# Modulation blocks in groups of four instead of two, in the gate-up chunks and the last down projection of a two-block transformer kernel

## The chip, the cores and the metric

The kernel runs on one core of one Trainium2 chip. The metric is the device time of one execution in microseconds (us). Engines: PE is TensorE (matmuls), ACT ScalarE, DVE VectorE, POOL GpSimd, SP the engine whose queue issues the weight DMAs.

## What is computed

Two model blocks run one after the other on 256 tokens of width 1024. The first has two layers (mixer, then a gated feed-forward network). The second has two layers whose norm is shifted, scaled and gated by "modulation" vectors. These depend only on two conditioning vectors, not on the tokens, so the kernel computes them while the first block is running. Cut to what matters:

```python
def hybrid_layer(x, ...):                       # first block, twice
    h = rms_norm(x, g_mix_pre)
    z = h @ w_in                                # mixer: retention, attention, gated MLP
    ...
    x = x + rms_norm(y @ w_out, g_mix_post)
    h = rms_norm(x, g_ffn_pre)
    gate, up = split(h @ w_gate_up, [FFN_HIDDEN])   # 1024 x 5632
    f = (silu(gate) * up) @ w_down                  # 2816 x 1024
    return x + rms_norm(f, g_ffn_post)

# second block, layer l: the modulation
mod_l = silu(c) @ w_mod[l] + b_mod[l]           # w_mod[l]: 1024 x 3072
mod_c = silu(c_ctx) @ w_mod[l] + b_mod[l]
sh, sc, g = split(mod, 3)                       # shift, scale, gate: the "thirds" 0, 1, 2
h = rmsnorm(x, norm_g[l]) * (1 + sc) + sh
```

## The kernel before

**Weights** come in one fixed order through a ring of 8 raw slots in SBUF, 512 KB each (`RAW = 8`). A piece of weights in a slot is a "granule". `ring` (filled at L357 to L411) is the order of the DMAs, which all stand in SP's queue: `load` (L434) issues the DMA of ring place i when the granule of place i − 8 has left its slot.

**Two kinds of granules.** A projection granule is cut into a high and a low part, so that three fast matmuls (high by high, low by high, high by low) stand for one of full precision. ACT writes the high part (`cut_high`, L447), DVE the low part (`cut_low`, L459), in ring order, three granules ahead of PE at most; four pairs of cut slots (`CUT = 4`) come free as PE finishes granules. The raw slot is free once the low part is cut. A modulation block (`add_mod`, L380) is one of eight 128-row input blocks of `w_mod` for one third. It is not cut: PE multiplies with the raw slot itself (`mod_rows_pe`, L985: four matmuls of 32 columns a block, recorded as 8), and the slot is free only when PE has done that (`mods_done`).

**Gate-up** (L3058 on): eleven chunks c of four granules h each. For each granule PE makes 12 matmuls of 512 columns (two token tiles, three products, two row blocks). At c ≥ 1, behind the granule h = 1, PE turns the f of chunk c − 1 (`turn_f`, L3047 to L3057, four transposes), after waiting for DVE to have formed it (`gate`, L2891 to L2903), which in its turn waits for ACT's tanh (`gate_tanh`, L2735 to L2743). In ACT's and DVE's order, tanh and gate of chunk c − 1 stand at the start of chunk c, which is behind the cut of the granule (c, 2): cuts run three granules ahead.

**Where modulation stands.** `MOD_AT` (L363) names granules (c, h) in gate-up at which blocks of third 0 stand. In the ring they come ahead of that granule (L377), on PE behind its matmuls (L3063). `MOD_LAST` (L388) names the down-projection granules n of layer 1 ahead of which blocks of third 2 stand, in the ring (L406) and on PE (L3091). Third 1 is at other places, in groups of four, among them the group of four behind the first gate-up chunk's second granule, and is not touched. When all eight blocks of third 0 are done, ACT copies the rows out (`mod_rows_act`, at c = 5), and DVE sums the gate rows at n = 10 of the last down projection.

**Other DMAs** near it: in layer 1, POOL fetches `ctx_raw` (1024 KB) when chunk 0 is done and `const_late` (1154 KB) when granule (2, 3) is done (L2660 to L2664).

Of the kernel before, what the change touches and what calls it, by code (L numbers as in the profile page):

```python
# [173 lines left out]
def program(nc, a, out, tables):  # L174
    where = Where()
    ctx = ExitStack()
    with ctx:
# [182 lines left out]
        PAIRS = [(2 * h, 2 * h + 1) for h in range(DK // 2)]  # L360
        IN_COLS = ((Z_GU, 2 * GMW), (Z_AQ, RW), (Z_AK, RW), (Z_AV, RW), (Z_RQ, RW), (Z_RK, RW), (Z_RV, RW), (Z_RG, RW))
        IN_CHUNKS, GU_CHUNKS = len(IN_COLS), FK // 2
        MOD_AT = {(2, 1): (0, 1), (2, 3): (2, 3), (4, 1): (4, 5), (4, 3): (6, 7)}  # L363
        w_in, w_out, w_gu, w_down, w_mods = [], [], [], [], {}

        def pre_gain(at, layer, rows):
            return vec_cols[:, at + layer * DK + rows[0]:at + layer * DK + rows[-1] + 1]
# [6 lines left out]
        def add_gu(layer, chunks):  # L374
            for c in chunks:
                for h, rows in enumerate(PAIRS):
                    if (c, h) in MOD_AT:  # L377
                        add_mod(layer, 0, MOD_AT[c, h])
                    w_gu[layer].add_split(a["w_gate_up"][layer], rows, c * SEQ, SEQ, pre_gain(V_FFN, layer, rows))

        def add_mod(layer, third, ks):
            ph = w_mods.setdefault((layer, third), Phase(f"mod{third}"))
            for k in ks:
                ph.add(a["w_mod_2"][layer], (k,), D * third, D, cut=False)


        FIRST_KS, LAST_KS = range(0, 4), range(4, 8)
        MOD_LAST = {4: (0, 1), 5: (2, 3), 7: (4, 5), 8: (6, 7)}  # L388
        MIX_ORDER = [(j, PAIRS[h]) for hs in ((2, 3), (1, 0)) for j in range(2) for h in hs]
        OUT_ORDER = [(j, PAIRS[h]) for hs in ((0, 1), (2, 3)) for j in range(2) for h in hs]  # L390
        for layer in range(DEPTH):
# [3 lines left out]
        for layer in range(DEPTH):  # L395
# [9 lines left out]
            for n in range(FK):  # L405
                if last and n in MOD_LAST:  # L406
                    add_mod(layer, 2, MOD_LAST[n])
                w_down[layer].add(a["w_down"][layer], (n,), 0, D)
# [573 lines left out]
        def gate_rows_bank(layer):  # L982
            return 5 if layer == DEPTH - 1 else 6

        def mod_rows_pe(e, third, ks, bank, parts=1):  # L985

            if third == 1 and ks[0] == 0:
                e.wait_ge(dve.sem, dve.value("ret_centred"))
            part = DK // parts
            for k in ks:  # L990
                g = w_mods[where.layer, third].granules[k]
                e.wait_ge(landed[g.slot], g.landed)
                for q in range(4):
                    last = e.matmul(PS[32 * q:32 * q + 32, bank, 0:SEQ], silu_c[:, k, :], g.raw[:, 0, q * SEQ:(q + 1) * SEQ],  # L994
                                    start=k % part == 0, stop=k % part == part - 1)
                last.then_inc(mods_done, 1)
# [1988 lines left out]
        def pe_layer(e, layer, cuts):  # L2985
# [63 lines left out]
            def turn_f(c):  # L3049

                e.wait_ge(dve.sem, dve.value(f"f{c}"))
                if c >= 2:
                    e.wait_ge(dve.sem, dve.value(f"f_L{c - 2}"))
                for kk in range(2):
                    for t in range(NT):
                        last = e.transpose(PS[:, TP[c % 2], kk * SEQ + t * P:kk * SEQ + (t + 1) * P],  # L3056
                                           f[:, c % 2, t, kk * P:(kk + 1) * P], ident)  # L3057
                last.then_inc(pe.sem, pe.mark(f"f_T{c}"))  # L3058
            for c in range(1, GU_CHUNKS):
                for h in chunk_pe(e, w_gu[layer].granules[4 * c:4 * c + 4], "gate_up", c, hT, MM[c % 2], lambda t: free_f(c)):  # L3060
                    if h == 1:
                        turn_f(c - 1)
                    if (c, h) in MOD_AT:  # L3063
                        mod_rows_pe(e, 0, MOD_AT[c, h], MOD_BANKS[0, 0])
                    elif (c, h) == (6, 2):
# [22 lines left out]
            for n, g in enumerate(g_down[:-4]):  # L3088
                if n == 2:
                    turn_f(GU_CHUNKS - 1)  # L3090
                if layer == DEPTH - 1 and n in MOD_LAST:  # L3091
                    mod_rows_pe(e, 2, MOD_LAST[n], gate_rows_bank(layer))
                if layer == DEPTH - 1 and n == 13:
# [55 lines left out]
def build(nc, arrays, tables):  # L3149
    a = {k: nc.dram_tensor(k, v.shape, mybir.dt.from_np(v.dtype), kind="ExternalInput").ap()  # L3150
         for k, v in arrays.items()}
    out = nc.dram_tensor("out", (1, SEQ, D), F32, kind="ExternalOutput").ap()
    program(nc, a, out, tables)
# [14 lines left out]
```

## Time and profile before

| | before |
|---|---|
| median of 3 runs | 1066.53 us (1066.33 to 1068.08) |
| profiled execution | 1066.61 us, span of the core 1064.7 us |
| granted TensorE clock, mean | 0.997 |
| PE busy | 1037.4 us, 97% |
| DVE, ACT, POOL busy | 64%, 52%, 8% |
| weight DMAs (queue q1) | 161.96 MB, 47.4% of the 16 DMA engines |
| `w_mod` DMAs | 48 of 512 KB each |
| L994 (modulation matmuls) | 384 records |

The page also gives the chain of work that ended last: PE has 87% of it. A row of a timeline reads: start, duration, engine, line, operation, written <- read tiles, how many were merged, and in brackets the idle time before it with what ended it. Matmuls overlap: the distance between the starts is what one costs. In a row of windows the last three numbers are the granted clock (1.00 is full), the busy share of the DMA engines and GB/s.

### The profile page before, as it was taken

How to read it: one execution, taken by the hardware profiler on the slowest of the kernel's cores; microseconds unless marked ns; L12 is line 12 of the kernel's file. 1: busy time of each engine (PE TensorE's matmuls, PEld its weight loads, DVE VectorE, ACT ScalarE, POOL GpSimd, SP SyncE). 2: the span in 40 equal slices, each digit the busy share in tenths (PEclk: the TensorE clock that was granted, in tenths of full speed). 3: DMA queues.
4: the chain of work that ended last, by engine and by line, in shares of the span. 5: the costliest groups of instructions: out<-in, count | busy, mean ns of one | idle time of the engine just before them, and what ended most of it. 6: DMA issues, size and time to landing. Idle time of an engine off the chain costs nothing.

```text
span 1064.7 us, 15796 instructions
## 1 busy us (share of the span) xinstructions
PE 1037.4 (97%) x6070; PEld 875.3 (82%) x6070; DVE 683.5 (64%) x1202; ACT 549.4 (52%) x998; POOL 83.9 (8%) x102
## 2 busy tenths in 40 slices
PE   7999999999999999999999999999998999999997
PEld 6899777788887999777788788899985678889785
DVE  5995676666546896675666357433457734986665
ACT  6665365555435565364655355334345734543772
POOL 2000110000002100110000001001000002220130
PEclk9999999999999999999999999999999999999999
DMA  9645576766666755586866585133131021542001
GB/s 346 204 144 163 192 258 222 247 205 188 190 195 233 225 155 163 193 284 214 296 222 187 188 302 154 45 102 122 60 99 38 1 80 40 178 158 80 2 2 40
DMA packets 103828, 170.75 MB, mean 160 GB/s; under 512 B 7365, under 2 KB 70866, under 8 KB 103498
## 3 DMA queue, kind: packets, MB, share of 16 engines
q1 hardware_dynamic: 101524, 161.96, 47.4%
q0 software_dynamic: 1696, 6.38, 1.9%
q10 hardware_dynamic: 534, 1.41, 0.3%
q8 instruction: 48, 0.79, 0.3%
q14 instruction: 26, 0.21, 0.1%
HBM read 168.21 MB, written 1.05 MB: 159 GB/s over the span
## 4 chain that ended last, share of the span: by engine, by line
PE 87%; DVE 7%; ACT 2%; issue 2%; DMA 1%; SPq 0%; DVEq 0%; POOLq 0%; POOL 0%; ACTq 0%
PE PS L492 17%; PE PS L497 16%; PE PS L493 16%; PE PS L3077 4%; PE PS L3081 4%; PE PS L3078 4%; PE PS L994 2%; PE PS L1873 2%; PE PS L960 1%; DVE low L462 1%; PE PS L961 1%; PE PS L965 1%; PE PS L1861 1%; PE PS L1984 1%; PE PS L3056 1%
## 5 line engine op out<-in xcount | busy, mean ns | idle before, releaser
L462 DVE TENSOR_TENSOR low<-raw,high 128x1024 fp32r<-128x1024 f32 (+3 forms) x182 | 202.3, 1117 | 167.1 <-ACT high L452 166.0
L492 PE MATMUL PS<-high,hT_high 128*128 128x512 f32 (+2 forms) x796 | 302.7, 381 | 0.3 <-ACT high L452 0.3
L493 PE MATMUL PS<-high,hT_low 128*128 128x512 f32 (+2 forms) x796 | 296.2, 372 | 0.0
L452 ACT ACTIVATE high<-raw 128x1024 fp32r<-128x1024 f32 (+3 forms) x186 | 179.3, 972 | 209.3 <-PE PS L497 114.9
L497 PE MATMUL PS<-low,hT_high 128*128 128x512 f32 (+2 forms) x796 | 231.9, 372 | 0.9 <-DVE low L465 0.9
L492 PEld LDWEIGHTS PS<-high,hT_high 128*128 128x128 f32 x796 | 150.2, 189 | 27.5 <-issue 5.1
L497 PEld LDWEIGHTS PS<-low,hT_high 128*128 128x128 f32 x796 | 147.5, 189 | 23.5 <-DVE low L465 2.1
L493 PEld LDWEIGHTS PS<-high,hT_low 128*128 128x128 f32 x796 | 150.5, 189 | 19.5
L465 DVE SCALAR_TENSOR_TENSOR low<-raw,vec_cols,high 128x512 fp32r<-128x512 f32 x176 | 123.7, 747 | 61.4 <-ACT high L455 61.4
L455 ACT ACTIVATE high<-raw,vec_cols 128x512 fp32r<-128x512 f32 x176 | 117.1, 715 | 59.4 <-PE PS L497 34.6
L3077 PE MATMUL PS<-high,fT_high 128*128 128x512 f32 x176 | 69.5, 395 | 0.0
L3078 PE MATMUL PS<-high,fT_low 128*128 128x512 f32 x176 | 68.7, 390 | 0.0
L3081 PE MATMUL PS<-low,fT_high 128*128 128x512 f32 x176 | 68.6, 390 | 0.0
L492 PE MATMUL PS<-high,cT_high 128*128 128x512 f32 (+2 forms) x124 | 45.2, 366 | 0.0
L493 PE MATMUL PS<-high,cT_low 128*128 128x512 f32 (+2 forms) x124 | 45.0, 365 | 0.0
L3077 PEld LDWEIGHTS PS<-high,fT_high 128*128 128x128 f32 x176 | 33.1, 188 | 8.3 <-issue 1.6
L3081 PEld LDWEIGHTS PS<-low,fT_high 128*128 128x128 f32 x176 | 33.1, 188 | 7.0
L3078 PEld LDWEIGHTS PS<-high,fT_low 128*128 128x128 f32 x176 | 33.1, 188 | 6.6
L497 PE MATMUL PS<-low,cT_high 128*128 128x512 f32 (+2 forms) x124 | 35.5, 365 | 0.0
L2433 DVE CUSTOM_DVE_ANT_0 z_late<-PS,consts 128x512 f32<-128x512 f32 x32 | 22.8, 749 | 15.8 <-PE PS L1995 15.8
L1962 ACT ACTIVATE z_late<-z_late,consts 128x512 f32<-128x512 f32 x32 | 22.9, 716 | 18.9 <-DVE consts L2433 18.9
L2747 ACT ACTIVATE fT_high<-PS 128x512 fp32r<-128x512 f32 x22 | 13.1, 598 | 37.5 <-PE PS L3056 37.5
(380 smaller groups left out, 1578.4 us busy)
## 6 DMA issues: line engine op xcount, KB each, us to landing
raw<-w_gate_up SPq DMA_DIRECT2D x176, 256.0 KB
raw<-w_mod SPq DMA_DIRECT2D x48, 512.0 KB
raw<-w_down SPq DMA_DIRECT2D x44, 512.0 KB
raw<-w_in SPq DMA_DIRECT2D x56, 384.0 KB
raw<-o_w_in SPq DMA_DIRECT2D x20, 512.0 KB
raw<-w_out SPq DMA_DIRECT2D x16, 512.0 KB
raw<-e_w_in SPq DMA_DIRECT2D x12, 512.0 KB
raw<-w_in SPq DMA_DIRECT2D x8, 512.0 KB
```

Of the source, the lines that this page charges most:

```text
L452: last = e.activation(g.high, g.raw, ACT.Copy)
L455: last = e.activation(g.high[:, i, :], g.raw[:, i, :], ACT.Copy, scale=g.gain[:, i:i + 1])
L462: last = e.tensor_tensor(g.low, g.raw, g.high.bitcast(F32), ALU.subtract)
L465: last = e.scalar_tensor_tensor(g.low[:, i, :], g.raw[:, i, :], g.gain[:, i:i + 1], g.high[:, i, :].bitcast(F32), ALU.mult, ALU.subtract)
L492: e.matmul(bank, xh[:, k, tokens], g.high[:, i, :], start=first and i == 0, stop=False)
L493: e.matmul(bank, xl[:, k, tokens], g.high[:, i, :], start=False, stop=False)
L497: done = e.matmul(bank, xh[:, k, tokens], g.low[:, i, :], start=False, stop=last and i == len(g.rows) - 1)
L1962: e.activation(o_prob[:, i % 4, :], o_logits[i % 4], ACT.Exp, bias=e_neg[:, i:i + 1], scale=-1.0, accum_out=e_den[:, i:i + 1]).then_inc(ac ...
L2433: e.tensor_tensor_reduce(o_logits[i % 4], PS[:, i % 2, :], late_const("window", NT)[:, t, :], -1.0, neg_sink[:, h:h + 1], ALU.add, ALU.min ...
L3077: e.matmul(bank, fT_high[:, n, tokens], g.high[:, 0, cols], start=n == 0, stop=False)
L3078: e.matmul(bank, fT_low[:, n, tokens], g.high[:, 0, cols], start=False, stop=False)
L3081: last = e.matmul(bank, fT_high[:, n, tokens], g.low[:, 0, cols], start=False, stop=n == FK - 1)
```

## The change

Two tables change. In `MOD_AT` the four groups of two blocks in the gate-up of each layer, at granules (2, 1), (2, 3), (4, 1) and (4, 3), become two groups of four at (2, 2) and (4, 2). In `MOD_LAST` the four groups of two in layer 1's down projection, at granules 4, 5, 7 and 8, become two groups of four at 5 and 8. The order of DMAs in SP's queue and the order of matmuls on PE follow from the same tables. Every block is still loaded and multiplied once, in the same order among themselves, into the same PSUM banks.

```diff
-        MOD_AT = {(2, 1): (0, 1), (2, 3): (2, 3), (4, 1): (4, 5), (4, 3): (6, 7)}
+        MOD_AT = {(2, 2): (0, 1, 2, 3), (4, 2): (4, 5, 6, 7)}
...
-        MOD_LAST = {4: (0, 1), 5: (2, 3), 7: (4, 5), 8: (6, 7)}
+        MOD_LAST = {5: (0, 1, 2, 3), 8: (4, 5, 6, 7)}
```

## Rows read from the trace of the kernel before

**Rows 1.** The page, part 1: engine, busy us, share of the span, instructions.
```profile
PE 1037.4 (97%) x6070; PEld 875.3 (82%) x6070; DVE 683.5 (64%) x1202; ACT 549.4 (52%) x998; POOL 83.9 (8%) x102
```
**Rows 2.** Waits of PE: who waited for whom, us in total, times, longest; then that wait's end.
```profile
PE PS L1065 <- DVE gel L1319: 2.9, 2, 2.2
...
51.11 1.22 PE L1065 MATMUL PS<-gel,wsT 128*128 128x128 f32 x4 [2.18 <-DVE gel L1319]
```
**Rows 3.** Timeline of PE, layer 0, chunks 2 and 3: turns, visits of two, granule starts.
```profile
166.98 0.60 PE L3056 MATMUL PS<-consts,f 128*128 128x128 f32 x4
...
171.38 0.39 PE L492 MATMUL PS<-high,hT_high 128*128 128x512 f32 x1
...
174.19 1.07 PE L994 MATMUL PS<-raw,silu_c 128*32 128x256 f32 x16
175.19 0.50 PE L492 MATMUL PS<-high,hT_high 128*128 128x512 f32 x1
...
178.09 0.39 PE L492 MATMUL PS<-high,hT_high 128*128 128x512 f32 x1
...
180.81 0.60 PE L3056 MATMUL PS<-consts,f 128*128 128x128 f32 x4
...
184.02 0.39 PE L492 MATMUL PS<-high,hT_high 128*128 128x512 f32 x1
```
**Rows 4.** Timeline of PE, layer 0, chunk 0: a visit of four blocks (third 1).
```profile
141.77 1.93 PE L994 MATMUL PS<-raw,silu_c 128*32 128x256 f32 x32
143.63 0.50 PE L492 MATMUL PS<-high,hT_high 128*128 128x512 f32 x1
```
**Rows 5.** Timeline of PE, layer 1, down projection: two visits with a granule between.
```profile
600.35 1.07 PE L994 MATMUL PS<-raw,silu_c 128*32 128x256 f32 x16
...
604.33 1.07 PE L994 MATMUL PS<-raw,silu_c 128*32 128x256 f32 x16
```
**Rows 6.** Timeline of SP, layer 1: the DMA issues behind the first visit.
```profile
487.82 3.95 SPq L444 DMA_DIRECT2D raw<-w_gate_up  x8
```
**Rows 7.** Timeline of PE, layer 1: first turn and visit, and chunk 3's turn.
```profile
486.60 0.60 PE L3056 MATMUL PS<-consts,f 128*128 128x128 f32 x4
487.12 1.07 PE L994 MATMUL PS<-raw,silu_c 128*32 128x256 f32 x16
...
511.80 0.60 PE L3056 MATMUL PS<-consts,f 128*128 128x128 f32 x4
```
**Rows 8.** Timeline of ACT, layer 1: cuts that waited for a DMA.
```profile
491.44 1.34 ACT L455 ACTIVATE high<-raw,vec_cols 128x512 fp32r<-128x512 f32 x2 [3.62 <-DMA raw<-w_gate_up]
...
505.73 2.66 ACT L455 ACTIVATE high<-raw,vec_cols 128x512 fp32r<-128x512 f32 x4 [4.07 <-DMA raw<-w_gate_up]
...
510.92 1.34 ACT L455 ACTIVATE high<-raw,vec_cols 128x512 fp32r<-128x512 f32 x2 [1.81 <-DMA raw<-w_gate_up]
...
612.40 1.06 ACT L452 ACTIVATE high<-raw 128x1024 fp32r<-128x1024 f32 x1 [3.01 <-DMA raw<-w_down]
```
**Rows 9.** Timeline of DVE, layer 1: the last step of chunk 3's f.
```profile
510.48 0.87 DVE L2902 SCALAR_TENSOR_TENSOR f<-f,norms,PS 128x256 f32<-128x256 f32 x2
```
**Rows 10.** Windows, us: busy by engine, clock, DMA share, GB/s; layer 1, then layer 0.
```profile
487.00:511.00 24.00, 24.00 (x131) 18.65 (x130) 12.29 (x20) 10.62 (x19) 1.09 (x2) 1.00 0.93 309
188.00:192.00 4.00, 4.00 (x20) 3.30 (x19) 3.30 (x7) 1.98 (x4) 0.00 (x0) 1.00 0.00 1
```
**Rows 11.** DMA queues from 494 to 504 us: packets, MB, share of 16 engines.
```profile
q0 software_dynamic: 176, 1.19, 46.5%
```
**Rows 12.** Windows behind PE's wait near 51 us.
```profile
51.10:54.50 3.40, 3.39 (x13) 3.40 (x14) 3.33 (x7) 1.26 (x2) 0.00 (x0) 0.50 0.40 116
54.50:58.00 3.50, 3.50 (x26) 3.47 (x26) 3.44 (x8) 1.97 (x4) 0.00 (x0) 1.00 0.45 119
```
**Rows 13.** Timelines of layer 0: the burst's second landing (ACT), chunk 3's turn (PE).
```profile
174.50 1.34 ACT L455 ACTIVATE high<-raw,vec_cols 128x512 fp32r<-128x512 f32 x2 [1.44 <-DMA raw<-w_gate_up]
...
192.18 0.60 PE L3056 MATMUL PS<-consts,f 128*128 128x128 f32 x4
```

## Prediction

> **What bounds the kernel now.** I read the page's busy times first: TensorE (PE) 97% busy, the vector and scalar engines far from that [rows 1]. Its waits, second, are few: the longest inside the run is 2.18 us at one place near 51 us [rows 2]. In the stretches that the change touches, the PE timeline has one matmul behind the other: from 178.09 to 180.81 us a "granule" (one 512 KB weight block: two token tiles by six matmuls) takes 2.72 us [rows 3]. So PE sets the end there. But the SP queue, the cuts on ACT and the DMA windows show that its cover is thin in one spot. That spot decides this change.
>
> All times are those of the profiled execution: span 1064.7 us, 1066.61 us with what lies around it; the median of the runs shown is 1066.53, so I take 0.1 off at the end. "g(c,h)" is granule h of gate-up chunk c, "m0" to "m7" are the eight modulation blocks of a phase.
>
> **The change, part by part.** Nothing is computed more or less: 48 blocks of modulation rows stand in the kernel before and after. In each layer's gate-up, two visits of PE with two blocks each (behind g(2,1) and g(2,3), and behind g(4,1) and g(4,3)) become one visit with four, behind g(2,2) and g(4,2). In the last down projection four visits become two.
>
> *A visit's price.* The first of a pair comes behind the turn of f (L3056), a visit of its own: from L3056 to the second granule's start 171.38 − 166.98 = 4.40 us; less 2.72 for the granule, 1.68. The turn alone costs 184.02 − 180.81 − 2.72 = 0.49 [rows 3], so these two blocks add 1.19. The second costs 178.09 − 171.38 − 2 × 2.72 = 1.27 [rows 3]. A visit of four is in the trace too, behind the first gate-up chunk: 143.63 − 141.77 = 1.86 us from its first matmul to the next granule's [rows 4], where two blocks take 175.19 − 174.19 = 1.00 [rows 3]. Two more blocks thus cost 0.86, and a visit of four 1.27 + 0.86 = 2.13. A merge in gate-up gives 1.19 + 1.27 − 2.13 = 0.33; there are four (two per layer): 1.3 us. In the down projection a visit costs 604.33 − 600.35 − 2.72 = 1.26 [rows 5], a merge gives 2 × 1.26 − 2.12 = 0.40, two of them 0.8. PE gains **2.1 us** in all.
>
> *What is moved in the queues.* A block's DMA into raw slot i may only be issued when the granule eight places earlier in the ring has left its slot. A weight granule leaves when DVE has cut it, some three granules ahead of PE; a modulation block leaves only when PE has multiplied with it. So SP stands at m0 until PE gets there, and everything behind m0 in SP's queue stands too. In layer 1 before: the turn starts at 486.60, m0's matmuls at 487.12, and SP sends a burst from 487.82 on, 0.70 us after them [rows 6, 7]. Afterwards g(2,2) stands between turn and m0: 486.60 + 0.49 + 2.72 + 0.09 (the entry: 174.19 − 171.38 − 2.72 [rows 3]) = 489.90 for m0, and the burst starts at 490.60, **2.78 us later**. And since four blocks now lie together, the order behind it changes. Before: g(3,1), g(3,2), g(3,3), g(4,0), m4, m5, g(4,1), g(4,2): g(4,2) is the 8th of the burst. After: g(3,2), g(3,3), g(4,0), g(4,1), m4 to m7, g(4,2): it is the **9th**.
>
> *Who waits for g(4,2).* ACT cuts its high part and only then takes chunk 3's tanh (L2742); DVE cuts its low part and only then forms f of chunk 3 (L2897, L2902); and PE turns that f (L3056) behind g(4,1), ahead of everything else. So its landing is behind the next turn, though no matmul of the granule itself is due. In layer 1 before, ACT waited for DMA until 505.73, when the 7th, g(4,1), came, and again until 510.92 for the 11th, g(4,3) [rows 8]: 5.19 / 4 = 1.30 us a block. The 8th hence landed near 507.03. f of chunk 3 was ready at 510.48 + 0.87 = 511.35 [rows 9], 4.32 us after that landing, and PE reached the turn at 511.80 [rows 7]: **0.45 us of margin**. Afterwards PE comes 0.33 earlier, 511.47. The 9th of a burst landed at 505.73 + 2 × 1.30 = 508.33, and 2.78 later is 511.11. f is ready at 515.43. PE waits **3.9 to 4.0 us**.
>
> *Bounds of that wait.* Low: the DMA engines were 0.93 busy over the whole burst [rows 10], partly with const_late, which POOL fetches at the end of chunk 2. If every block took 1.30 us behind a first landing 491.44 − 487.82 = 3.62 us after issue [rows 6, 8], and const_late (1154 KB) 2.25 such shares, the 9th would land at 490.60 + 3.62 + 10.4 + 2.9 = 507.5 and the wait would be 0.4 us. High: one more share of 1.30, if const_late, which does not move with the burst, gets in the way more: 5.3 us. I take 3.9, because the same queue with the same guest has shown just this rate at this place.
> The Trainium skill says (DMA: Bandwidth & Descriptors, "Issuing engines are not separate DMA queues") that DMAs from different engines run on the same 16 DMA engines and interleave. The trace agrees: const_late's queue q0 had 46.5% of the engine time from 494 to 504 us [rows 11]. With engines of its own it would give those 4.65 us back, g(4,2) would land near 506.5, f would be ready before PE comes, and only the gain would be left.
>
> *The clock.* Such a wait can cost more than itself. PE's wait of 2.18 us up to 51.11 [rows 2] is followed by 3.40 us at a granted clock of 0.50, that is 1.2 GHz in place of 2.4, then 1.00 again [rows 12]. Half of 3.40 us of matmuls is lost, **1.7 us**. A wait of 3.9 us is longer than that one; between nothing and twice 1.7, I take 1.7.
> The Trainium skill (TensorE: Matmul & The Clock Gate, "HAM oscillation — how this bites in real kernels") describes this very course: a wait for DMA, the clock falls, the next piece of work starts at the low one. It speaks against this change, and the rows above bear it out once.
>
> *The other places.* The same wait in layer 0 has no const_late beside it. Its burst's 2nd block landed at 174.50, and by 188 the queue was empty (0.00 DMA share from 188 to 192) [rows 10, 13], so 1.30 to 1.40 a block. The 9th, 2.78 later, lands at 174.50 + 7 × (1.30 to 1.40) + 2.78 = 186.4 to 187.1, f is ready at 190.7 to 191.4, and PE comes at 192.18 − 0.33 = 191.85 [rows 13]. No wait, 0.4 to 1.1 us of margin; below, a miss of one share would cost up to 0.9. The second merge of each layer, behind g(4,2), delays its burst alike, but what is due first there is g(5,2), now the burst's first block: landing 3.6 us after m4 is done, f 4.3 later, against 1.3 + 3 × 2.72 = 9.5 us until PE's turn: 1.6 us to spare. In the down projection m5 now waits for m0 one granule longer (2.7 us), but granule 8 moves from 5th to 4th in that burst. It landed at 612.40 [rows 8]; I bound it afterwards by 612.40 and 612.40 + 2.7 − 1.3 = 613.8; with its cut it is ready at 613.5 to 614.9, and PE wants it at 600.3 + 4 × 2.72 + 2 × 2.12 = 615.4, less the 0.2 (178.09 − 175.19 − 2.72 [rows 3]) that a visit costs only inside the next granule, 615.2 [rows 5]: cost 0, at most 0.5 for its low part. The wait sits on PE, and behind it stand all its matmuls; nothing later in the trace is late enough to absorb it.
>
> *Sum:* 1066.6 − 2.1 + 3.9 + 1.7 = 1070.1, against the median **1070.0 us**.
>
> **The rivals.** *A wait without the clock's fall*, or a shorter wait than 2.2 us: 1066.6 − 2.1 + (0.4 to 3.9) = 1064.9 to 1068.4. For it: DMA could run nearer to its 1.30 us share from the start. Against: it did not at this place. *The gain alone* (the other side, faster): g(4,2) lands by 507.1, all waits stay away: 1066.5 − 2.1 = 1064.4, and with merges worth 0.40 everywhere 1064.1. It decides at a landing of 511.47 − 4.32 = 507.15, nearly 4 us ahead of what the burst's rate gives. For it speaks that no matmul of the change waits; against it, that the margin is 0.45 us now. *More waits*: layer 0's turn or the down projection waits too, or the low clock lasts twice as long: 1072 to 1074. *That the merges give nothing* (a visit's price is in the blocks): 141.77 to 143.63 excludes it, as four blocks took 1.86 and not 2.00; it would only shift all cases by 2.
>
> **How the numbers follow.** Wait with the clock's fall 0.60, its own range 1068.7 to 1072.0; wait without it or a short one 0.21; the gain alone 0.13; more waits 0.06. Measurement can tell about 0.2% (2.1 us) from no change, so the bounds are 1064.4 and 1068.7. Faster: half of the gain-alone case, 0.07. Slower: the first and the last case, 0.65. Same: 0.28. The range 1065.0 to 1072.0 leaves out the gain alone and most of the last case, some 0.18.
>
> **What would show it.** The visits: L994 in visits of 32 matmul records, 1.86 us from the first to the next granule. The queue: in layer 1 SP's burst behind m0 near 490.6 (less what layer 0 gained), ACT's idle time ahead of g(4,2)'s cut until about 511 and ended by DMA raw<-w_gate_up. The wait: one new idle stretch of PE near 4 us ahead of L3056 in layer 1, put down to DVE f, and a granted clock of 0.50 for some 3.4 us behind it. In layer 0 no idle time of PE at L3056. I am wrong if g(4,2) lands before 507.2, or if PE's turn in layer 1 follows without idle time.

## The result, and the profile after

| | before | after |
|---|---|---|
| median of 9 runs each, us | 1066.86 (1066.0 to 1068.2) | 1069.29 (1067.57 to 1070.69) |
| profiled execution, us (span) | 1066.61 (1064.7) | 1067.57 (1065.6) |
| granted clock, mean | 0.997 | 0.997 |

The ratio is 1.0024, 95% interval 1.0016 to 1.0033: the change makes the kernel 2.4 us slower. The profiled execution is the quickest of the nine, so its own difference to before is only 1.0 us; where the rest lies is told below.

PE's waits in the changed kernel, the page's view of who waited for whom (us in total, times, longest). The fourth line is new:

```profile
PE PS L3125 <- DMA consts<-const_early: 3.2, 1, 3.2
PE PS L1065 <- DVE gel L1319: 2.9, 2, 2.2
PE PS L1798 <- DVE z_late L1920: 2.8, 7, 0.6
PE PS L3056 <- DVE f L2902: 2.6, 1, 2.6
```

It is one wait, at the place that was named: chunk 3's turn in layer 1 (a "turn" is the group of four transposes at L3056). Four timelines of the changed kernel show how it comes about, in order. SP's burst behind the first visit, after PE's visit of four at 488.18:

```profile
488.18 1.93 PE L994 MATMUL PS<-raw,silu_c 128*32 128x256 f32 x32
```
```profile
488.88 3.95 SPq L444 DMA_DIRECT2D raw<-w_gate_up  x8
492.88 3.15 SPq L444 DMA_DIRECT2D raw<-w_mod  x4
496.07 9.84 SPq L444 DMA_DIRECT2D raw<-w_gate_up  x8
```

Four gate-up granules (eight DMAs), then four modulation blocks, then g(4,2): it is the ninth. ACT, where the cut of g(4,2) waits for it and chunk 3's tanh stands behind the cut; DVE, where f stands behind the low cut; and PE, whose last two matmuls of g(4,1) start at 509.25:

```profile
508.12 1.34 ACT L455 ACTIVATE high<-raw,vec_cols 128x512 fp32r<-128x512 f32 x2 [5.70 <-DMA raw<-w_gate_up]
509.36 0.82 ACT L2742 ACTIVATE f_tanh<-PS,norms 128x256 f32<-128x256 f32 x2
```
```profile
511.54 0.87 DVE L2902 SCALAR_TENSOR_TENSOR f<-f,norms,PS 128x256 f32<-128x256 f32 x2
```
```profile
509.25 0.61 PE L497 MATMUL PS<-low,hT_high 128*128 128x512 f32 x2
512.46 0.66 PE L3056 MATMUL PS<-consts,f 128*128 128x128 f32 x4 [2.59 <-DVE f L2902]
```

Before, the same f was ready at 511.35 and PE came at 511.80 [rows 7, 9]. Two windows of the changed kernel, the columns as in [rows 10] (the third number from the end is the granted clock):

```profile
487.00:488.80 1.80, 1.80 (x18) 1.13 (x20) 1.41 (x2) 0.35 (x1) 0.00 (x0) 1.00 0.00 0
488.80:509.60 20.80, 20.80 (x115) 16.60 (x104) 7.84 (x13) 8.09 (x14) 1.09 (x2) 1.00 0.97 344
...
513.40:516.90 3.50, 3.50 (x10) 2.70 (x9) 3.50 (x6) 1.57 (x3) 0.00 (x0) 0.51 0.00 0
```

The DMA engines stand idle (share 0.00) while SP waits for m0, and then are 0.97 busy until g(4,2) is there. Behind the wait the clock is at 0.51 for some 3.4 us.

**The ledger of the profiled pair.** The turns (L3056) are good marks. In the changed kernel (the turn at 512.46 stands above):

```profile
154.36 0.60 PE L3056 MATMUL PS<-consts,f 128*128 128x128 f32 x4
165.73 0.60 PE L3056 MATMUL PS<-consts,f 128*128 128x128 f32 x4
179.18 0.60 PE L3056 MATMUL PS<-consts,f 128*128 128x128 f32 x4
190.75 0.66 PE L3056 MATMUL PS<-consts,f 128*128 128x128 f32 x4
204.26 0.60 PE L3056 MATMUL PS<-consts,f 128*128 128x128 f32 x4
...
484.90 0.60 PE L3056 MATMUL PS<-consts,f 128*128 128x128 f32 x4
498.34 0.60 PE L3056 MATMUL PS<-consts,f 128*128 128x128 f32 x4
...
527.56 0.60 PE L3056 MATMUL PS<-consts,f 128*128 128x128 f32 x4
...
596.25 0.60 PE L3056 MATMUL PS<-consts,f 128*128 128x128 f32 x4
...
630.83 1.91 PE L781 MATMUL PS<-consts,e_ctx_normed 128*128 128x128 f32 x16
```

Those of the kernel before that [rows 3, 7, 13] don't hold:

```profile
155.61 0.60 PE L3056 MATMUL PS<-consts,f 128*128 128x128 f32 x4
...
206.02 0.60 PE L3056 MATMUL PS<-consts,f 128*128 128x128 f32 x4
...
500.43 0.60 PE L3056 MATMUL PS<-consts,f 128*128 128x128 f32 x4
...
525.64 0.60 PE L3056 MATMUL PS<-consts,f 128*128 128x128 f32 x4
...
594.33 0.60 PE L3056 MATMUL PS<-consts,f 128*128 128x128 f32 x4
...
629.81 1.91 PE L781 MATMUL PS<-consts,e_ctx_normed 128*128 128x128 f32 x16
```

| stretch | before, us | after, us | difference |
|---|---|---|---|
| layer 0, turn 1 to 2 (first merge) | 180.81 − 166.98 = 13.83 | 13.45 | −0.38 |
| layer 0, turn 2 to 3 | 192.18 − 180.81 = 11.37 | 11.57 | +0.20 |
| layer 0, turn 3 to 4 (second merge) | 13.84 | 13.51 | −0.33 |
| layer 1, turn 1 to 2 (first merge) | 13.83 | 13.44 | −0.39 |
| layer 1, turn 2 to 3 (the wait) | 11.37 | 14.12 | +2.75 |
| layer 1, turn 3 to 4 (second merge, low clock) | 13.84 | 15.10 | +1.26 |
| layer 1, last turn to e_ctx's turn (down projection, two merges) | 35.48 | 34.58 | −0.90 |

That makes +2.2 us for the change. The +0.20 in layer 0 is a small wait too: f was ready at 189.82 + 0.87 = 190.69, and PE, due at 190.55, turned it at 190.75; the view of waits shows nothing of it. The other −1.25 us stand ahead of the change's first place: layer 0's turn of chunk 0 is at 154.36 where it was at 155.61. In the profile of before, a low clock followed the wait near 51 us [rows 12]; in this one the same wait, 2.18 us long again, was followed by none. The medians, 2.4 us apart, depend less on that chance.

### The profile page after: what moved, and what is told of

The parts are those of the page before. It is cut to its first block, busy times and chain, and to the rows that moved or that the text cites. A ratio compares the mean times of both kernels' runs of the same rounds, so it can differ in the third digit from the quotient of the medians.

```text
span 1065.6 us, 15796 instructions
## 1 busy us (share of the span) xinstructions
PE 1035.9 (97%) x6070; PEld 874.2 (82%) x6070; DVE 682.7 (64%) x1202; ACT 548.4 (51%) x998; POOL 83.9 (8%) x102
## 4 chain that ended last, share of the span: by engine, by line
PE 81%; DVE 9%; DMA 4%; issue 3%; ACT 3%; SPq 0%; DVEq 0%; POOLq 0%; POOL 0%; ACTq 0%
PE PS L492 15%; PE PS L497 15%; PE PS L493 15%; PE PS L3077 4%; PE PS L3081 4%; PE PS L3078 4%; DMA raw<-w_gate_up 3%; PE PS L994 2%; DVE low L462 2%; PE PS L1873 2%; PE PS L960 1%; PE PS L961 1%; PE PS L965 1%; PE PS L1861 1%; PE PS L1984 1%
## 5 line engine op out<-in xcount | busy, mean ns | idle before, releaser
L497 PE MATMUL PS<-low,hT_high 128*128 128x512 f32 (+2 forms) x796 | 231.7, 372 | 1.0 <-DVE low L465 1.0
L497 PEld LDWEIGHTS PS<-low,hT_high 128*128 128x128 f32 x796 | 147.3, 188 | 23.9 <-DVE low L465 2.2
L497 PE MATMUL PS<-low,cT_high 128*128 128x512 f32 (+2 forms) x124 | 35.5, 365 | 0.0
L2433 DVE CUSTOM_DVE_ANT_0 z_late<-PS,consts 128x512 f32<-128x512 f32 x32 | 22.8, 749 | 15.9 <-PE PS L1995 15.8
L1461 ACT ACTIVATE xn<-PS 128x512 f32<-128x512 f32 (+1 forms) x56 | 29.3, 526 | 0.0
```

The lines of the kernel that those rows point to most:

```text
L497: done = e.matmul(bank, xh[:, k, tokens], g.low[:, i, :], start=False, stop=last and i == len(g.rows) - 1)
L1461: return e.activation(dst, src, ACT.Copy, **({} if scale is None else {"scale": scale}))
```

## The experiments

Theory 1 is the chain above: where the group stands sets when SP's burst begins and at which place of it g(4,2) comes; const_late fills the DMA engines beside it; f, and with it PE's turn, waits; a low clock may follow. Rival A: groups of four are dear by themselves, wherever they stand. Others are named as they come. Each kernel was run beside the kernel before on the same chip, and "faster" and "slower" are worked out from the ratio to it.

**e1 and e2: the two tables apart.** e1 changes `MOD_LAST` only, e2 `MOD_AT` only.

```diff
 # e1
-        MOD_LAST = {4: (0, 1), 5: (2, 3), 7: (4, 5), 8: (6, 7)}
+        MOD_LAST = {5: (0, 1, 2, 3), 8: (4, 5, 6, 7)}
 # e2
-        MOD_AT = {(2, 1): (0, 1), (2, 3): (2, 3), (4, 1): (4, 5), (4, 3): (6, 7)}
+        MOD_AT = {(2, 2): (0, 1, 2, 3), (4, 2): (4, 5, 6, 7)}
```

> Only the down projection's visits are merged (two fewer); gate-up keeps its pairs. Theory 1 (the loss is one wait of TensorE in layer 1's gate-up, 2.6 us, with the low clock that may follow, 1.7 us): no wait comes in, the merges give 2 x 0.40, so 0.8 us faster than before, near 1066.0. Rival A (a visit of four is itself dearer, or the longer hold of raw slots costs in the down projection too): 0 to 2 us slower than before.

Measured: 1066.16 us, ratio 0.9994 (0.9985 to 1.0003). That agrees with −0.8 us and with no change, and excludes a loss above 0.3 us. Its profile also held a surprise: with pairs in gate-up, as before, PE waited at the same turn.

```profile
506.87 2.69 ACT L455 ACTIVATE high<-raw,vec_cols 128x512 fp32r<-128x512 f32 x4 [6.02 <-DMA raw<-w_gate_up]
...
512.56 0.66 PE L3056 MATMUL PS<-consts,f 128*128 128x128 f32 x4 [0.75 <-DVE f L2902]
```

Here the burst began at 487.00 and its 7th block came at 506.87, 19.9 us later; in the profile of before it was 505.73 − 487.82 = 17.9 [rows 6, 8]. The DMA's rate differs between executions by more than the margin of 0.45 us, so the arrangement of before waits now and then itself. The turns show more than the waits do: from turn 2 to turn 3 of layer 1 this profile took 12.95 us where undisturbed ones take 11.37, so 1.6 us were lost, 0.75 and another 0.3 of them as waits in the view. The distance between starts is the better measure.

> Only the gate-up visits are merged; the down projection keeps its pairs. Theory 1: as the changed kernel without the down projection's 0.8 us: 3 us slower than before (2.6 wait, 1.7 clock, less 1.3 for four merges), near 1070, with TensorE idle for 2 to 4 us ahead of chunk 3's turn in layer 1 and nowhere else. Rival A: half of the loss or less, since half of the new visits of four are taken away with the down projection's.

Measured: 1069.72 us, ratio 1.0033 (1.002 to 1.0045), 3.5 us slower. The loss is all in gate-up. That it is larger than the changed kernel's by what the down projection gives agrees with the medians, within their intervals; the traces show that gift directly, 34.6 us from the last turn to e_ctx's in every profile with the merged down projection and 35.5 in those with pairs. In the profile the wait was 4.0 us, and the low clock twice as long:

```profile
509.82 1.33 ACT L455 ACTIVATE high<-raw,vec_cols 128x512 fp32r<-128x512 f32 x2 [8.75 <-DMA raw<-w_gate_up]
...
514.16 1.12 PE L3056 MATMUL PS<-consts,f 128*128 128x128 f32 x4 [4.01 <-DVE f L2902]
```
```profile
513.10:519.90 6.80, 5.74 (x16) 4.55 (x16) 5.54 (x10) 3.04 (x5) 0.00 (x0) 0.50 0.01 3
```

The last row is a window of that kernel: clock 0.50 over 6.8 us, the first 1.1 of them still inside the wait. PE also waited 0.34 us at chunk 2's turn in layer 0 (179.69), which the forecast "nowhere else" had not.

**e3 and e4: the guest.** The "guest" is const_late, which shares the DMA engines with SP's burst. POOL fetches it, and the 8 KB of o_sink behind it, at the end of chunk 6; e3 in the changed kernel, e4 in the kernel before.

```diff
-                e.wait_ge(granules_done, w_gu[DEPTH - 1].granules[11].cut + 1)
+                e.wait_ge(granules_done, w_gu[DEPTH - 1].granules[27].cut + 1)
                 e.dma_start(consts[:, late_at:late_at + late_width], a["const_late"])...
```

> The changed kernel, and POOL fetches const_late (1154 KB) at the end of layer 1's chunk 6 rather than chunk 2. Theory 1 with the guest transfer as a needed part: granule (4,2) lands some 4.6 us earlier than 508.1, f of chunk 3 is ready before TensorE comes, no wait, and only the gain of the merges is left: 2.1 us faster than before, near 1064.7. Rival B (the later burst and the ninth place are enough by themselves, const_late does not matter): the wait stays at 2 us or more and the kernel 2 us slower than before.

Measured: 1063.47 us, ratio 0.9973 (0.9962 to 0.9985), 2.9 us faster than before. The wait is gone but for 0.16 us (turn 2 to turn 3 took 510.50 − 498.97 = 11.53 us, not 11.37):

```profile
506.15 1.34 ACT L455 ACTIVATE high<-raw,vec_cols 128x512 fp32r<-128x512 f32 x2 [4.73 <-DMA raw<-w_gate_up]
...
509.57 0.87 DVE L2902 SCALAR_TENSOR_TENSOR f<-f,norms,PS 128x256 f32<-128x256 f32 x2
...
510.50 0.66 PE L3056 MATMUL PS<-consts,f 128*128 128x128 f32 x4
```

The burst began at 489.51, so g(4,2) took 506.15 − 489.51 = 16.6 us in place of 508.12 − 488.88 = 19.2. So the guest costs it 2.6 us in this pair. As the pace differs between executions, one pair is thin evidence, but layer 0 has the same burst without a guest: there it took 186.40 − 169.71 = 16.7 us in the changed kernel's profile, 16.0 in e2's, 16.6 in e5's and 15.8 in e8's, while the five bursts with the guest (table below) took 18.8 to 20.7. The means, 16.3 (with e3's) and 19.6, differ by 3.2 us; the single values allow 2.1 to 4.9. That is most likely less than the 4.65 that the guest's share of engine time in [rows 11] would give. Rival B (the guest does not matter) falls.

> The kernel before with const_late fetched at the end of chunk 6: the control for e3. Theory 1: TensorE did not wait in this stretch before, so nothing changes, within 0.3 us of before. Rival C (moving const_late is worth time by itself, so that e3 would say nothing on the groups): 1 us or more faster.

Measured: 1066.33 us, ratio 0.9999 (0.999 to 1.0007). In its profile f of chunk 3 was ready at 509.32 and PE came at 512.05, a margin of 2.7 us instead of 0.45. Moving the transfer alone is worth nothing that shows, so e3's gain is that of the merges with their hindrance gone.

**e5 and e6: the layers apart.** `MOD_AT` becomes a pair of tables, one per layer; in e5 layer 0 has groups of four, in e6 layer 1; the down projection has its pairs.

```diff
+        MOD_AT = ({(2, 2): (0, 1, 2, 3), (4, 2): (4, 5, 6, 7)},
+                  {(2, 1): (0, 1), (2, 3): (2, 3), (4, 1): (4, 5), (4, 3): (6, 7)})      # e5; e6 the other way
...
-                    if (c, h) in MOD_AT:
-                        add_mod(layer, 0, MOD_AT[c, h])
+                    if (c, h) in MOD_AT[layer]:
+                        add_mod(layer, 0, MOD_AT[layer][c, h])
```

> Gate-up visits merged in layer 0 only; layer 1 and the down projection keep their pairs. Theory 1: no wait of TensorE of more than 0.2 us at chunk 3's turn (f was ready 0.06 us ahead of it in the changed kernel), two merges at 0.33 less some 0.1: 0.5 us faster than before, near 1066. Rival A (groups of four hurt in both layers alike): 1 us or more slower.

> Gate-up visits merged in layer 1 only. Theory 1: the whole loss is here: 2.6 us of wait and up to 1.7 us of low clock less 0.66 us, 3.6 us slower than before, near 1070.2. Rival A: 1 to 2 us slower, half of the loss in each layer.

Measured: e5 1066.38 us, ratio 1.0001 (0.9992 to 1.0009): the 0.5 us of gain that was forecast can't be told from nothing. Its profile shows no wait of PE at a turn in layer 0 (turn 2 to turn 3 took 0.13 us more than 11.37 there), but one of 0.73 us in layer 1, with pairs there, as e1; that stretch took 12.43 us, 1.1 more than undisturbed. e6 1070.32 us, ratio 1.0032 (1.0021 to 1.0043), 3.4 us slower: layer 1 carries the whole loss. This fells rival A twice over: the same groups of four cost nothing in the down projection, and in layer 0 a few tenths of a microsecond in some profiles (0.1 to 0.5), less than the 0.8 that the two merges there give.

**e7: the same groups, one granule later.**

```diff
-        MOD_AT = {(2, 2): (0, 1, 2, 3), (4, 2): (4, 5, 6, 7)}
+        MOD_AT = {(2, 3): (0, 1, 2, 3), (4, 3): (4, 5, 6, 7)}
```

> All merges kept, but gate-up's groups of four stand at the last granule of their chunks, (2,3) and (4,3), rather than at the third. Theory 1, with the place in the burst as its core: granule (4,2) moves from ninth to fourth in the burst that TensorE's visit releases. The burst begins 2.7 us later still, but the granule that chunk 3's f waits for comes some 5 x 1.3 us earlier in it: no wait, 2.1 us faster than before, near 1064.6. Rival D (it is the later start of the burst that makes the wait, whatever the order): the wait grows by up to 2.7 us, 4 us or more slower than before.

Measured: 1063.99 us, ratio 0.9979 (0.9971 to 0.9988), 2.2 us faster. In its profile:

```profile
491.64 4.51 SPq L444 DMA_DIRECT2D raw<-w_gate_up  x8
496.20 4.88 SPq L444 DMA_DIRECT2D raw<-w_mod  x4
...
498.38 0.60 PE L3056 MATMUL PS<-consts,f 128*128 128x128 f32 x4
...
500.48 2.76 ACT L455 ACTIVATE high<-raw,vec_cols 128x512 fp32r<-128x512 f32 x4 [8.96 <-DMA raw<-w_gate_up]
...
508.56 0.88 DVE L2902 SCALAR_TENSOR_TENSOR f<-f,norms,PS 128x256 f32<-128x256 f32 x2
...
510.71 0.60 PE L3056 MATMUL PS<-consts,f 128*128 128x128 f32 x4
```

The burst begins 2.8 us after that of the changed kernel, later than in every kernel so far, and yet f is ready at 509.44, 1.3 us ahead of PE: g(4,2) is now among its first four granules. Rival D (only the start counts) falls. What const_late now meets is the burst's head: ACT stood 8.96 us for g(3,3), and PE waited 0.2 us for its low part (L497 in chunk 3), its one wait in the view. The turns show that this costs more: 510.71 − 498.38 = 12.33 us, 0.96 above the undisturbed 11.37. So the place removed the wait for f, and most of the loss, but not all of it.

**e9: the same groups, one granule earlier**, `MOD_AT = {(2, 1): (0, 1, 2, 3), (4, 1): (4, 5, 6, 7)}`.

> All merges kept, gate-up's groups of four behind the second granule of their chunks, (2,1) and (4,1). The burst in layer 1 begins as early as before, but granule (4,1) is its ninth and (4,2) its tenth. Theory 1 (start of the burst plus place times 1.3 us): (4,2) lands 2.7 us less 1.3 us, so 1.4 us, earlier than in the changed kernel against TensorE; waits in chunk 4 of layer 1, split between the cut of (4,1) and f of chunk 3, of 1 to 2.5 us in all, and more rarely a low clock: 1 us slower than before to 1 us faster, near 1066.5. Rival D (only the start of the burst counts): no wait, 2 us faster. Rival F (only the place counts): a wait of 4 us or more, 2 to 4 us slower than before.

Measured: 1066.57 us, ratio 0.9997 (0.9988 to 1.0005), as forecast. The waits of PE, in its profile, between 480 and 530 us:

```profile
PE PS L3056 <- DVE f L2902: 0.8, 1, 0.8
PE PS L492 <- ACT high L455: 0.8, 1, 0.8
PE PS L497 <- DVE low L465: 0.2, 1, 0.2
```
```profile
499.35 0.60 PE L3056 MATMUL PS<-consts,f 128*128 128x128 f32 x4
...
513.31 0.66 PE L3056 MATMUL PS<-consts,f 128*128 128x128 f32 x4 [0.80 <-DVE f L2902]
```

The second block is from PE's timeline. PE waited 1.8 us in three pieces, and none was followed by a low clock there. By the turns, 513.31 − 499.35 = 13.96 us, the stretch lost 2.6 us, hardly less than the changed kernel's 2.75, as the ninth block of this execution's burst came 507.57 − 487.16 = 20.4 us after its start. So the profile does not show the shorter wait that was forecast; the times do: e9 is 2.1 us below the changed kernel beside it (e11), and rivals D and F fall by the same times. Start of the burst and place in it both count: ninth and tenth in an early burst is better than ninth in a late one, and fourth in a still later one better than either.

**e10: both remedies**, the table of e7 and the later const_late of e3.

> Both remedies: groups of four at the last granule of their chunks and const_late fetched at the end of chunk 6. Theory 1: either remedy alone already takes the wait away, so the second gives nothing: as e7 or e3, 2.4 to 3.1 us faster than before, near 1063.7. Rival G (e7 still loses something to const_late, and e3 something to the ninth place): 1 us faster than either.

Measured: 1063.31 us, ratio 0.9969 (0.9958 to 0.998), 3.3 us faster than before and 5.3 us faster than the changed kernel beside it (e11). Its profile has no wait of PE in the gate-up of layer 1, and f of chunk 3 is ready 2.7 us ahead of its turn (DVE, then PE):

```profile
506.07 0.87 DVE L2902 SCALAR_TENSOR_TENSOR f<-f,norms,PS 128x256 f32<-128x256 f32 x2
```
```profile
498.30 0.60 PE L3056 MATMUL PS<-consts,f 128*128 128x128 f32 x4
...
509.67 0.60 PE L3056 MATMUL PS<-consts,f 128*128 128x128 f32 x4
```

Its interval overlaps those of e3 and e7, so the times alone do not show that the second remedy adds 0.4 to 1.1 us. The turns speak for it: 509.67 − 498.30 = 11.37 us here, where e7 took 12.33 and e3 11.53. That either remedy alone takes the whole loss away, as forecast, is true of e3 to 0.16 us and not of e7.

**e8: the clock.** Ten needless matmuls ahead of the turn keep PE busy in its wait:

```diff
             def turn_f(c):
+                if layer == 1 and c == 3:
+                    e.wait_ge(dve.sem, dve.value(f"f_L{c - 2}"))
+                    for _ in range(10):
+                        e.matmul(PS[:, TP[c % 2], :].rearrange("p (k s) -> p k s", k=2),
+                                 hT_high[:, 0, 0:P], hT_high[:, 0:2, :], start=True, stop=True)
                 e.wait_ge(dve.sem, dve.value(f"f{c}"))
```

> The changed kernel, with ten needless matmuls of 512 columns (2.3 us, results overwritten) ahead of chunk 3's turn in layer 1, where TensorE stands idle for 2.6 us. Theory 1 for the clock: the wait stays as long, but it no longer looks idle, so the low clock of 3.4 us behind it goes: 0 to 1.7 us faster than the changed kernel, 0.7 to 2.4 us slower than before, near 1068. Rival E (the clock behind the wait costs nothing here, or falls anyway): the same time as the changed kernel, 2.4 us slower than before, or slower still by the matmuls.

Measured: 1067.88 us, ratio 1.0015 (1.0006 to 1.0024). In its profile (the turn is L3061 here):

```profile
509.27 2.43 PE L3054 MATMUL PS<-hT_high 128*128 128x512 f32 x10
512.53 0.66 PE L3061 MATMUL PS<-consts,f 128*128 128x128 f32 x4 [0.83 <-DVE f L2902]
```
```profile
513.00:517.00 4.00, 4.00 (x38) 2.79 (x40) 4.00 (x7) 1.82 (x3) 0.00 (x0) 1.00 0.00 0
```

PE's turn comes no sooner than in the changed kernel (3.3 us late by the turns, where that was 2.75), but the clock stays at 1.00 behind it. e8's median is 1.5 us above before on its chip; the changed kernel's are 1.7 (e11, below) and 2.4 us above theirs. That is a gain of 0.2 to 0.9 us with overlapping intervals. The granted clocks of all runs say the same: none of e8's eleven runs has a mean below 0.996, of the changed kernel's 21 runs nine have. So the sign is likely and the size open; rival E is made unlikely, not excluded.

**e11: the changed kernel again**, on the chip of e9 and e10.

> The changed kernel again, beside e9, e10 and the kernel before on this chip. Theory 1: a wait ahead of chunk 3's turn in layer 1 whose length differs from run to run with the DMA's rate (2.1 to 4.0 us in the profiles so far), followed or not by 3.4 us of low clock: 1067.5 to 1071, median 2.4 us slower than before. Rival A: 1068 to 1069.5 without such a spread, beyond that of the kernel before.

Measured: 1068.64 us, ratio 1.0019 (1.0008 to 1.0029), twelve runs from 1066.3 to 1071.2, while 23 runs of before beside them lay between 1065.4 and 1068.3. In its profile the wait at the turn was 2.76 us, and this time a low clock followed both it and the wait near 51 us:

```profile
52.30:55.50 3.20, 3.20 (x11) 3.18 (x11) 3.16 (x5) 1.26 (x2) 0.00 (x0) 0.50 0.42 119
513.10:516.30 3.20, 2.69 (x9) 2.31 (x10) 3.20 (x7) 2.21 (x5) 0.00 (x0) 0.50 0.00 0
```

All profiles with groups of four behind g(2,2) in layer 1, from SP's burst to ACT's start on g(4,2), with PE's wait, the low clock by it, and how much longer than 11.37 us turn 2 to turn 3 took:

| kernel | burst, us | g(4,2), us | between | PE's wait | turn late | low clock |
|---|---|---|---|---|---|---|
| changed | 488.88 | 508.12 | 19.24 | 2.59 | 2.75 | 3.4 |
| e11, the same | 489.86 | 509.26 | 19.40 | 2.76 | 2.92 | 3.4 |
| e2 | 489.15 | 509.82 | 20.67 | 4.01 | 4.17 | 6.8 |
| e6 | 490.26 | 509.05 | 18.79 | 2.15 | 2.31 | none |
| e8, with filler | 488.44 | 508.18 | 19.74 | 0.83 | 3.26 | none |
| e3, const_late later | 489.51 | 506.15 | 16.64 | none | 0.16 | none |

The turn's lateness follows the burst's length one for one: it is that length less 16.5 us in all six, the kernels with the filler and without the guest included.

## Why the prediction was right

The forecast was 1070.0 us in a range of 1065.0 to 1072.0, with slower at 0.65. Measured: 1069.29. Point by point:

- **The gain of the merges** was put at 0.33 us each in gate-up and 0.40 in the down projection, 2.1 in all. The ledger shows 0.38 and 0.39 for the first of each layer and 0.45 each in the down projection, which makes 2.5 in all at four and two merges. So the term was a little small. The kernels without the large wait (e3, e7, e10) are 2.9, 2.2 and 3.3 us faster than before. What e3 and e10 gain beyond 2.5 us is open. It is not that before pays for its thin margin now and then: e4, which has 2.7 us of margin, is no faster than before beyond noise. Part of it goes with the clock: the mean granted clock of their runs is 0.0003 to 0.0007 above that of before beside them, which is 0.3 to 0.7 us of the span.
- **The burst's shift**, forecast 2.78 us. From turn 1 to the burst it was 487.82 − 486.60 = 1.22 us [rows 6, 7] and is 488.88 − 484.90 = 3.98: 2.76.
- **The ninth place** is there in SP's rows, and e7, fourth place in a burst later still, shows that it matters.
- **From landing to f**, forecast 4.32 us: 511.54 + 0.87 − 508.12 = 4.29.
- **The landing** was the term that was sized too high: 20.5 us after the burst's start, where it was 19.2. So the wait was 2.6 us, not 3.9. This is the mis-sized term of the sum. The step took one execution's pace of 1.30 us a block, and the same arrangement has since given 18.8 to 20.7 us. A spread of 2 us should have stood beside that number. The upper end, 4.0 us, did occur.
- **The guest** was held to cost 4.65 us, from its share of engine time, so that without it f would be ready before PE comes. e3 shows 2.6, the means of all bursts 3.2. That the wait vanished all the same, but for 0.16 us, was luck: the guest was sized 2.0 us too high and the landing 1.3 us too late, and the two errors nearly cancelled.
- **The clock**, forecast 1.7 us on top. In the changed kernel's profile it was 15.10 − (13.84 − 0.38) = 1.64 us. But it was treated as one fixed term where it is a draw: after waits of 2.6 and 2.8 us it fell, by one of 4.0 it was low for 6.8 us, after 2.15 it did not fall. Near 51 us PE waited 1.9 to 2.2 us in all thirteen profiles, and the clock fell for 3.4 us behind that in seven of them (before, e3, e4, e6, e7, e9, e11) and in six not. This, with the length of the wait, spreads the changed kernel's runs over 3 to 5 us where those of before spread over some 2 to 3: its four runs of 1070.4 us and more have mean clocks of 0.993 and 0.994, the other five 0.995 to 0.997. As the sum was made against a profile that held such a fall of its own, it could as well have been 1.7 us off.
- **Layer 0** was put at no wait with 0.4 to 1.1 us of margin. The turn came 0.2 us late there. This is a small miss in the other direction: g(4,2) landed 16.7 us behind the burst's start, where 1.30 to 1.40 us a block from the second landing on had given 0.6 to 1.3 us less. The bound that stood beside it, up to 0.9 us for a miss of one share, held.
- **The down projection** was put at no new wait, and there was none.

The likeliest case was the one that came, with its wait 1.3 us shorter: by its own terms the sum would then have been 1068.7, 2.2 us above before, and the ledger's 2.2 us and the medians' 2.4 us agree. Some of that closeness is luck: the merges gave 0.4 us more than their term, small waits took 0.3 back, and the size of the clock's term is one draw.

## What to carry to other kernels

Suppose a stream of loads runs through a ring of buffers, and one piece in it is held until it is used. Before moving that piece, ask which loads queue behind it and who waits first for those, and not only whether the piece itself is in time. Here the first to wait was a step two engines further on. A group of held pieces is best placed so that what is next due comes first in the burst that it releases: the same merge was 2.4 us slower at one granule, 2.2 us faster at the next. Look for other transfers that start at the same point of the program: moving one away turned the loss of 2.4 us into a gain of 2.9.

## What the runs showed of the hardware

- A low clock (0.50, 1.2 GHz) can follow a wait of TensorE of 2.2 us, and need not: in the same place, after waits of 1.9 to 2.2 us, it fell in seven of thirteen profiles. By waits of 2.6 to 2.8 us it lasted 3.4 us, by one of 4.0 us 6.8 us. It began between 1.1 us before the wait's end (e2) and 1.2 us behind it (e11, near 51 us). No long wait is needed either: in e9's profile one more low clock of 3.4 us stands at 816.5 us, behind four waits of only 0.2 to 0.6 us between 811 and 816. With ten needless matmuls in the wait it stayed at 1.00 in e8's profile. The Trainium skill (TensorE: Matmul & The Clock Gate, "HAM oscillation — how this bites in real kernels") tells of such falls behind waits for DMA; these rows agree in kind, though the waits here were for VectorE: at the turn it had itself waited for a DMA, near 51 us the view names its own work (`gel`).
- A queue of 512 KB loads, with the DMA engines 0.93 to 0.97 busy, ran at paces that differed by 10% between the profiles of five kernels with the same order of loads there (18.8 to 20.7 us for nine blocks and a guest of 1154 KB), and by 11% up to the seventh block in before, e1 and e5, which have the same order too (17.9, 19.9 and 19.4 us).
- Visits of TensorE to matmuls of 32 columns among matmuls of 128 cost 0.38 to 0.45 us apiece beside their own work. The Trainium skill (TensorEngine Tiling (Array Packing), "Key Properties") says that a change of tiling mode drains the engine. The rows agree that a visit has a price, but don't tell such a drain apart from the change of weights and data type that goes with it here.
